# Second block's mixer: weight pieces in gaps 0 to 3, last values and the result's turning inside the out pieces, four banks for the turning

## The reference, cut to what matters

```
h = rms_norm_2(x, norm_mix)                 # 256 x 1024
q, k, v, u, g = split(h @ w_in)             # 5 x 512 columns
a  = dilated_attention(rotary(q), rotary(k), v)       # 8 heads of 64, 3 merged bands
sg = gelu(u) * (w_s @ layer_norm(gelu(g)) + b_s)      # spatial gating, 2 chunks of 128 tokens
mixed = concat[rms_norm(a, g_attn), rms_norm(sg, g_sgu)]
x = x + mixed @ w_out                       # 1024 x 1024
```

## Time and profile before

| what | value |
|---|---|
| median of 3 runs | 2006.92 us (2003.07 to 2007.05) |
| the profiled execution, its own time | 2009.89 us |
| its span, first to last instruction | 2007.7 us |
| PE busy | 1890.5 us (94%) |
| DVE busy | 1353.8 us (67%) |
| ACT busy | 1096.7 us (55%) |
| mean granted TensorE clock | 0.967 |
| DMA | 228 GB/s mean over the span |

### The profile page before, as it was taken

How to read it: one execution, slowest core, us unless ns; L and a number is a source line. 1 busy time by engine, 2 the same in 40 slices (tenths; PEclk the granted TensorE clock), 3 DMA queues, 4 the chain that set the end, 5 groups by cost and what they waited for, 6 DMA issues and landing times.

```text
span 2007.7 us, 27018 instructions
## 1 busy us (share of the span) xinstructions
PE 1890.5 (94%) x11125; PEld 1619.8 (81%) x11125; DVE 1353.8 (67%) x1772; ACT 1096.7 (55%) x1452; POOL 49.0 (2%) x52
## 2 busy tenths in 40 slices
PE   4988899999899799999899999899999999989998
PEld 2845688888686688888799987799989998769997
DVE  2687688888876598888855556466566555546655
ACT  3433577777666477777644446454445444545443
POOL 0000010000000010100000000000000000000000
PEclk9989899999999799999999999899999999989999
DMA  9567599999869299999945555245555555425551
GB/s 366 189 221 293 177 334 325 329 343 325 326 215 332 94 344 312 335 340 327 320 147 189 189 185 166 84 148 190 194 188 184 189 188 187 145 84 168 189 189 53
DMA packets 209322, 456.98 MB, mean 228 GB/s; under 512 B 8848, under 2 KB 20776, under 8 KB 209192
## 3 DMA queue, kind: packets, MB, share of 16 engines
q1 hardware_dynamic: 204800, 450.99, 64.7%
q10 hardware_dynamic: 4392, 4.18, 0.6%
HBM read 454.09 MB, written 1.05 MB: 227 GB/s over the span
## 4 chain that ended last, share of the span: by engine, by line
PE 88%; DVE 5%; ACT 4%; issue 1%; DMA 1%; POOL 0%; SPq 0%; ACTq 0%; DVEq 0%; POOLq 0%
PE bank L297 86%; PE bank L1940 2%; DVE rest L633 1%; DVE arena L1222 1%; DMA raw<-in_mod_w 1%; DVE arena L1230 1%; PE bank L2208 1%; ACT round L616 0%; ACT arena L742 0%; DVE small L1222 0%; ACT hTh L774 0%; DVE xres L1222 0%; DVE hTl L1222 0%; DVE htokl L1222 0%; ACT arena L1155 0%
## 5 line engine op out<-in xcount | busy, mean ns | idle before, releaser
L633 DVE TENSOR_TENSOR rest<-raw,round 128x1024 fp32r<-128x1024 f32 (+1 forms) x760 | 888.9, 1218 | 267.4 <-ACT round L616 267.3
L616 ACT ACTIVATE round<-raw 128x1024 fp32r<-128x1024 f32 (+1 forms) x760 | 758.9, 1050 | 405.5 <-PE bank L297 391.5
L297 PE MATMUL bank<-hTh,round 128*128 128x256 f32 x1600 | 450.5, 282 | 17.0 <-DVE hTl L1222 13.1
L297 PE MATMUL bank<-hTh,rest 128*128 128x256 f32 x1600 | 448.5, 280 | 0.0
L297 PE MATMUL bank<-hTl,round 128*128 128x256 f32 x1600 | 448.4, 280 | 0.0
L297 PEld LDWEIGHTS bank<-hTh,round 128*128 128x128 f32 x1600 | 303.2, 190 | 23.3 <-issue 20.8
L297 PEld LDWEIGHTS bank<-hTh,rest 128*128 128x128 f32 x1600 | 305.3, 191 | 0.0
L297 PEld LDWEIGHTS bank<-hTl,round 128*128 128x128 f32 x1600 | 303.6, 190 | 1.0 <-issue 0.2
L297 PE MATMUL bank<-round,hTh 128*128 128x512 f32 x464 | 186.9, 403 | 6.8 <-DVE hTl L1222 3.1
L297 PE MATMUL bank<-round,hTl 128*128 128x512 f32 x464 | 183.3, 395 | 0.0
L297 PE MATMUL bank<-rest,hTh 128*128 128x512 f32 x464 | 182.5, 393 | 0.0
(11 more groups left out here) (220 smaller groups left out, 2197.4 us busy)
## 6 DMA issues: line engine op xcount, KB each, us to landing
raw<-in_ex_w SPq DMA_DIRECT2D x192, 1024.0 KB, 5.7
raw<-in_mod_w SPq DMA_DIRECT2D x48, 1024.0 KB, 7.4
raw<-in_ffn_w_gate SPq DMA_DIRECT2D x44, 1024.0 KB, 5.1
raw<-in_ffn_w_up SPq DMA_DIRECT2D x44, 1024.0 KB, 5.1
raw<-in_ffn_w_down SPq DMA_DIRECT2D x44, 1024.0 KB, 4.8
raw<-in_w_in SPq DMA_DIRECT2D x20, 1024.0 KB, 5.1
raw<-in_ev_in_w SPq DMA_DIRECT2D x10, 1024.0 KB, 13.0
raw<-in_od_in_w SPq DMA_DIRECT2D x8, 1024.0 KB, 7.0
```

The source lines that it names most:

```text
L297: return e.matmul(o, l, r, start=start, stop=stop, skip_group_check=True)
L616: e.activation(hi[:, h], raw[:, h], ACT.Copy).then_inc(S("hi"), 1)
L633: e.tensor_tensor(lo[:, h], raw[:, h], hi[:, h].bitcast(F32), ALU.subtract).then_inc(S("lo"), 1)
```

## The change

On all three engines `SIDE` becomes (1, 1, 1, 1, 2, 0, 1, 0): the v pieces stand in steps 0 and 1, the u pieces in steps 2 and 3, both y in step 4, nothing in step 5, the turning of the gated part in step 6, nothing in step 7. The out pieces leave `rest()`. PE now issues turn_p(7), pv(6), o0 with pv(7) between its two token halves, and o1 with the turning of the attention half between its two token halves, then o2 and o3. The attention half is turned through four banks (6, 7, 4, 5) instead of two, so that none of PE's chunks waits for an earlier one. ACT and DVE follow: ACT computes the gated part's squares after turn_p(7) and into another scratch area (`m_g` instead of `sq2`, which shares its place with `m_o`); DVE computes the mean square, the reciprocal and the product with it before `out_x` of o0.

```diff
-SIDE = (1, 1, 0, 1, 1, 2, 1, 1)
+SIDE = (1, 1, 1, 1, 2, 0, 1, 0)
 # ACT, rest(): after stage 6
-                    e.wait_ge(S("sgu_u"), 2 * l + 2)
-                    squares(m_u, sq2, 104, S("on_sq"))
-                    yield
                     half_turned(1, (2, 3))
-                    yield
-                    act_split(e, ahead, W.where["w_out_2", (l,), 512, 0])
-                    yield
-                    act_split(e, ahead, W.where["w_out_2", (l,), 512, 512])
                     yield
 # ACT, after the loop
-                next(side)
                 turn_p(7)
-                next(side)
-                half_turned(0, (6, 7))
+                act_split(e, ahead, W.where["w_out_2", (l,), 512, 0])
+                e.wait_ge(S("sgu_u"), 2 * l + 2)
+                squares(m_u, m_g, 104, S("on_sq"))
+                act_split(e, ahead, W.where["w_out_2", (l,), 512, 512])
+                half_turned(0, (6, 7, 4, 5))
 # DVE, rest(): mean_square(104) and out_half(1, nh) leave it; after the loop
-                next(side)
-                next(side)
+                split_to(W.where["w_out_2", (l,), 512, 0])
+                e.wait_ge(S("on_sq"), 2 * l + 1)
+                mean_square(104, 2, 512).then_inc(S("on_ms"), 1)
                 e.wait_ge(S("mix_e"), 8 * l + 8)
                 own.did(e.reciprocal(den, den))
...
-                half_turned(0, (6, 7))
+                out_half(1, 0)
+                split_to(W.where["w_out_2", (l,), 512, 512])
+                half_turned(0, (6, 7, 4, 5))
+                out_half(1, 1)
 # PE
-                        if cc >= 2:
+                        if cc >= len(among):
                             e.wait_ge(S("cat_lo"), 8 * l + 4 * (1 - part) + cc - 1)
...
-                def out_half(part, nh):
+                def out_half(part, nh, between=None):
...
+                        if th == 0 and between is not None:
+                            between()
...
+                turn_p(7)
                 pv(6)
-                next(side)
-                turn_p(7)
-                next(side)
-                pv(7)
-                e.wait_ge(S("mix_o"), l + 1)
-                e.wait_ge(S("mix_P"), 8 * l + 8)
-                half_turned(m_o, 0, (6, 7))
+
+                def result_turned():
+                    e.wait_ge(S("mix_o"), l + 1)
+                    half_turned(m_o, 0, (6, 7, 4, 5))
+
+                out_half(1, 0, lambda: pv(7))
+                out_half(1, 1, result_turned)
                 for nh in range(2):
                     out_half(0, nh)
```

More of the change, by code:

```diff
@@ L1123, in half_turned @@
                         e.wait_ge(S("cat_T"), 8 * l + 4 * (1 - part) + cc + 1)
-                        e.activation(catT[0][:, 4 * part + cc, :], banks[among[cc % 2]][:, 0:T], ACT.Copy,
+                        e.activation(catT[0][:, 4 * part + cc, :], banks[among[cc % len(among)]][:, 0:T], ACT.Copy,
                                      scale=col[:, l * 4 + cc:l * 4 + cc + 1]).then_inc(S("cat_hi"), 1)
@@ L1819, in rest @@
                         yield
-                    e.wait_ge(S("on_sq"), 2 * l + 1)
-                    mean_square(104, 2, 512).then_inc(S("on_ms"), 1)
-                    yield
                     half_turned(1, (2, 3))
                     yield
-                    for nh in range(2):
-                        out_half(1, nh)
-                        yield
                 def half_turned(part, among):
@@ L1833, in half_turned @@
                         e.wait_ge(S("cat_hi"), 8 * l + 4 * (1 - part) + cc + 1)
-                        stt(lo, banks[among[cc % 2]][:, 0:T], col[:, l * 4 + cc:l * 4 + cc + 1], hi.bitcast(F32),
+                        stt(lo, banks[among[cc % len(among)]][:, 0:T], col[:, l * 4 + cc:l * 4 + cc + 1], hi.bitcast(F32),
                             ALU.mult, ALU.subtract).then_inc(S("cat_lo"), 1)
@@ L2525, in half_turned @@
                     for cc in range(4):
-                        if cc >= 2:
+                        if cc >= len(among):
                             e.wait_ge(S("cat_lo"), 8 * l + 4 * (1 - part) + cc - 1)
                         for th in range(2):
-                            ins = tr(banks[among[cc % 2]][:, th * 128:(th + 1) * 128], src[:, th, cc * 128:(cc + 1) * 128])
+                            ins = tr(banks[among[cc % len(among)]][:, th * 128:(th + 1) * 128], src[:, th, cc * 128:(cc + 1) * 128])
                         ins.then_inc(S("cat_T"), 1)
-                def out_half(part, nh):
+                def out_half(part, nh, between=None):
                     i, k, views = take("w_out_2", (l,), part * 512, nh * 512)
```

## The result

The changed kernel takes 1978.51 us (median of 4 runs, 1973.74 to 1983.30) against 2005.59 us (4 runs, 2003.07 to 2007.05); the ratio is 0.9865, 95% interval 0.9843 to 0.9887. Two later comparisons, with six runs of this kernel each, gave 0.9898 (0.9866 to 0.9929) and 0.9897 (0.9872 to 0.9923), medians 21.6 and 21.8 us apart instead of 27.1. The profiled execution took 1983.30 us, 26.6 less than the one of before (forecast: 26.9 less).

A forecast was written before the change was run, and what follows sets the result against it. PE (busy 94%) bounds the kernel, losing time only at two waits per mixer and the low clock behind them. Gains 11.9 + 10.6 + 4.4 = 26.9 us take the profiled 2009.89 to 1983.0; median forecast 1981, range 1976 to 1991.

The forecast's parts named there:

- Where PE stands still: Each mixer: PE waits 3.07 us at the gated part's turning and 4.35 before o2, with low clock after each.
- Early steps: Steps 0 to 3: pieces one gap earlier cost 0, at most 0.5 us for v's banks; pv(3) ends as before.
- Turning: Gated part's turning, steps 5 to 7: PE stalls of 0.7, 0.1 and 0.25, together 1.1 us per layer instead of 3.07.
- Tail: From turn_p(5) to o2's start: 17.5 us work, 0.4 for small/wide changes, 1.1 stalls, together 19.0.
- Cover: Slack of DVE's work before PE wants it: attention half's chunks 0.9 us before o2, product with the reciprocal 4.2.
- The clock: o2's first 11 matmuls ran at low clock; 2.2 us per layer given back if no wait precedes o2.
- The whole time: Whole kernel: profiled execution 1983.0 us, median less the same sum 1980.0; 1981 given, chance 0.55.
- the 3.07: PE's wait in us at the gated part's turning in the first layer before the change; predicted to shrink to 1.1 of stalls.
- the second place: Attention half's turning before o2: PE waits 2.35, 0.87 and 1.13 us, 4.35 in all, then low clock; predicted to go.
- Rival 1: Clock falls in the mixer's tail, costing 2.7 to 4.6 us per layer: 1985 (one layer) or 1989 (both); chance 0.33.
- Rivals 2, 3 and 4: Turning keeps its wait, about 1994 us (0.07); low clock through tail, about 2013 (0.03); early pieces wait, no gain (0.02).
- Rival 3: Slower: low clock from the gated part's turning to o2 and beyond, some 26 us, giving about 2013 us; chance 0.03.

The follow-up runs named there:

- e2: Changed kernel with the side work back in its old steps, the new tail and the squares' new place kept; 1980.46 us, ratio 0.9887 to the kernel before.
- e3: Kernel before the change with only its side work moved to the new steps, old tail kept; 1998.53 us, ratio 0.9968.
- e6: Changed kernel with ACT's squares back ahead of the gated part's turning, done three times over, results unused; profiled mixer stretches 84.86 and 86.99 us.
- e7: Changed kernel with the attention half turned through two banks (6, 7) instead of four; profiled mixer stretches 78.92 and 78.91 us.
- e8: Changed kernel with the attention half turned after o1 instead of between its token halves; profiled mixer stretches 80.14 and 79.37 us.
- e5: Changed kernel with ACT's squares of the gated part back ahead of its turning, once; profiled mixer stretches 77.84 and 77.83 us.
- e1: Changed kernel run again with no edit; 1981.79 us, ratio 0.9898 to the kernel before.
- e11: Changed kernel run a third time with no edit; 1984.21 us, ratio 0.9897 to the kernel before.
- e9: Changed kernel with the gated part's turning split in two stages, plus PE's first v piece ahead of the first scores; 1985.08 us, ratio 0.9891 to the kernel before.

## Why the prediction was right

Right, and by its own steps. **Where PE stands still**: e2, e3, e6, e7 and e8 confirm that the two waits and the low clock behind them are what is gained; DVE's and ACT's busy times are unchanged within 0.2%. **Early steps** at no charge: from the first scores to the end of pv(3) it is 39.02 us (1232.62 to 1271.64) and was 39.03. v's banks held nothing up.

**Turning**: waits 0.87 and 0.34, together 1.2, against 0.7, 0.1 and 0.25, together 1.1. The order of what is late was right too: turn_p(7) waits for DVE's soft(7) behind the chunks, which e5 shows. **Tail**: 19.0 was forecast from the turning to o2; it is 19.5 in both layers (1271.64 to 1291.17, 1755.50 to 1775.03). The waits are 0.1 of the difference; the term of the work and of the changes between small and wide matmuls, 17.9, was 0.4 too small. **Cover**: DVE's last chunk was forecast 0.9 before o2. DVE's queue in the first layer shows the product (line 1217 here), o0's additions, the split of o3 and the four chunks (line 1225 here):

```profile
1281.74 1.42 DVE L1217 TENSOR_TENSOR arena<-bank,small 128x256 f32<-128x256 f32 x4
1285.06 1.41 DVE L1225 SCALAR_TENSOR_TENSOR xres<-bank,small,xres 128x512 f32<-128x512 f32 x2 [1.90 <-PE bank L297]
1286.38 2.35 DVE L633 TENSOR_TENSOR rest<-raw,round 128x1024 fp32r<-128x1024 f32 x2
1288.65 1.65 DVE L1225 SCALAR_TENSOR_TENSOR catTl<-bank,cols,catTh 128x256 fp32r<-128x256 f32 x4
```

The chunks end at 1290.30, 0.9 before o2. The product is done at 1283.2, 4.4 before the turning (forecast 4.2).

**The clock**: o2's low clock gave back 2.2 in the first layer and 2.1 in the second (forecast 2.2): from o2 to the feed-forward 21.06 became 18.90, and 20.96 became 18.91. Gains against the forecast: first layer 13.6 (14.1), second 13.8 (12.8), where 1.65 are the shorter low clock at its start that the prediction kept outside its sum; without it 12.1. Sum 27.3 against 26.9, with errors of -0.5 and -0.7 and one chance of 1.65 that nearly cancel: that the sums agree within 0.4 is in part luck.

**The whole time.** The median was forecast at 1981; it is 1978.51, and 1981.79 and 1984.21 in e1 and e11. Measured against the kernel before beside them, e1 and e11 gain 21.6 and 21.8 us, 5 less than the sum forecast; at 0.9866 and 0.9872 their intervals reach 26.8 and 25.7. The traces show the 27 us in the mixers, but the kernel before was profiled once. Where the other 5 us go is open.

**What was argued and turned out otherwise.** The prediction did not say which edit carries the gain. Each taken out of the changed kernel by itself, the edits are worth: the steps -0.3 per layer (e2), the squares' place 0.35 (e5), four banks 1.4 (e7), the turning inside o1 1.9 (e8). These do not add up to the 13.6 of the first layer, since steps and squares stand in for each other: what they remove together, the 3.07 less 1.2 of wait and the clock behind it (4.6 and 3.5 in e6), is 6.5 us there, about as much as the second place (4.35 of waits and 2.2 of clock). **Rival 1** (clock falls in the tail) had 0.33. It happened in none of the six layers of the changed kernel (first profile, e1, e11), and in one of the ten with a wait of 0.87, at 0.8 and not 2.7 to 4.6. After 1.23 to 1.26 of wait it fell in one layer of six (e2, e3, e5), for 10.2 us; after e8's 1.65 in neither of two; after e9's 2.3 in both. So the length of the wait alone does not decide it. The page "TensorE: Matmul & The Clock Gate" of the Trainium skill, section "A second HAM failure mode: psum-queue depth-cycling", says that short idles between groups can make the clock swing; the traces agree that they can, in one layer of ten and of six at these lengths. **Rivals 2, 3 and 4** did not show. (Rival 3 was argued from a longest low stretch of 10.2; e6 has one of 13.7.)

## What to carry to other kernels

Behind a wait of the matrix engine count the low clock too. The same 8 transposes, 16 value matmuls and 12 wide ones behind the 3.07 took 10.15 and 8.85 in the two layers before, and 5.6 at full clock in e2: 4.6 and 3.3 more. And a change that only shortens the wait can miss or win that part by chance (e3). Small work that hangs on other engines belongs inside a wide one, between two halves of it, with as many banks as it has chunks: that made the gain at the second place, about half of the whole. At the first place it was the queue's order, and either of two edits would have made most of it, so take out each edit alone before you say what it is worth. Where one in-order queue serves several chains, move the queue's items before the work: cutting the turning in two stages gave 1.6 per layer more, and moving a large piece ahead (e9) lost more than the wait that it shortened.

## What the runs showed of the hardware that was not expected

The same feed-forward stage, 1274 matmuls without a wait and at full clock, takes either 179.0 or 175.8 us, sometimes 175.0, and which one changes from stage to stage and from run to run. There are four such stages. The windows of the first 175.8 us of the first two of them, before and after; look at the number of matmuls in the second column.

```profile
1013.80:1189.60 175.80, 175.80 (x1261) 165.68 (x1262) 105.79 (x115) 80.16 (x98) 0.72 (x1) 1.00 0.56 186
1325.20:1501.00 175.80, 175.80 (x1275) 164.87 (x1276) 108.44 (x119) 82.73 (x100) 0.69 (x1) 1.00 0.57 191
```

```profile
1015.40:1191.20 175.80, 175.80 (x1275) 164.88 (x1276) 108.50 (x119) 81.33 (x99) 0.72 (x1) 1.00 0.58 191
1310.10:1485.90 175.80, 175.80 (x1261) 165.68 (x1262) 105.62 (x115) 81.54 (x99) 0.69 (x1) 1.00 0.55 186
```

In the slow ones the matmuls of 256 columns start 0.118 us apart nearly throughout, in the fast ones 0.113 in part of the groups; those of 512 columns are 0.229 apart in both. Before, the four stages took 179.0, 175.8, 179.0, 175.8; after, 175.8, 179.0, 175.0, 179.0. Four such stages are 13 us between all fast and all slow, which is the size of the spread of one kernel's runs (1978.76 to 1990.58 in e1). The first block, which no edit touches, varies too: the first of these stages begins at 1011.6 to 1020.1 us of the span in the thirteen profiles. So a comparison of times of this kernel below some 4 us needs many runs, while the mixer stretch repeats to 0.05. What sets the pace was not found: the clock granted is 1.00 in all of them, and no wait is recorded. That these two things explain the spread of the timed runs is likely and not shown, as only profiled runs have a trace.
